# Gates of three branches as 1024-column panels, three of eight k pairs by seven block products, on one core

## What is computed

```python
h = rms_norm(x, norm_g)
u = h @ w_in                       # 7752 columns of branches, then 4 x 2048 columns of gates
...                                # y_a, y_b, y_c, y_m: four mixers of width 512
gate_all = gates.reshape(B, S, N_BRANCH, D_MODEL)
for n, (y, z) in enumerate(((y_a, a_z), (y_b, b_z), (y_c, c_z), (y_m, m_z))):
    branch = y.reshape(B, S, W).astype(dt) * jax.nn.silu(z)
    merged = merged + jax.nn.sigmoid(gate_all[:, :, n]) * (branch @ w_branch[n])
return x + merged @ w_out
```

## Time and profile before

| | |
|---|---|
| median of 3 runs | 3312.29 us (3312.0 to 3312.94) |
| the profiled execution | 3312.98 us, span of its instructions 3311.2 us |
| granted TensorE clock | 0.999 |
| matmuls on PE | 15262, busy 3293.0 us |
| DVE, ACT, POOL busy | 1884.9, 1511.4, 279.0 us |
| DMA | 619.71 MB, mean 187 GB/s |

### The profile page before, as it was taken

The page is one execution under the profiler, slowest core; times in us unless marked ns, Lnnn a source line. Parts: engine busy times, 40 slices in busy tenths (PEclk is TensorE's granted clock), DMA queues, the critical chain, the costliest instruction groups (busy, mean ns, idle before and its releaser), DMA issues.

```text
span 3311.2 us, 39162 instructions
## 1 busy us (share of the span) xinstructions
PE 3293.0 (99%) x15262; PEld 2733.0 (83%) x15262; DVE 1884.9 (57%) x2068; ACT 1511.4 (46%) x1906; POOL 279.0 (8%) x237
## 2 busy tenths in 40 slices
PE   8999999999999999999999999999999999999999
PEld 7888888888888888888888888888888888888887
DVE  5466655555555656555555555575555555555555
ACT  5454445444444444454444445455444444444443
POOL 0111240000000102400000011160000000000000
PEclk9999999999999999999999999999999999999999
DMA  8665555666666655556666675554665666666665
GB/s 296 193 197 165 160 173 164 205 194 193 190 197 204 179 171 159 171 166 188 207 192 189 193 214 172 171 179 141 197 186 189 188 191 192 192 188 191 192 192 167
DMA packets 324279, 619.71 MB, mean 187 GB/s; under 512 B 24960, under 2 KB 29440, under 8 KB 322944
## 3 DMA queue, kind: packets, MB, share of 16 engines
q1 hardware_dynamic: 324096, 617.22, 62.1%
HBM read 609.80 MB, written 7.34 MB: 186 GB/s over the span
## 4 chain that ended last, share of the span: by engine, by line
PE 61%; DVE 0%; issue 0%; ACT 0%; ACTq 0%
PE G L900 57%; PE PT L662 2%; PE PO L773 1%; PE PS L745 1%; PE PS L747 0%; PE G L894 0%; PE PS L800 0%; PE PS L799 0%; PE PO L766 0%; PE PS L821 0%; DVE arena L1194 0%; PE PO L810 0%; ACT w_hi L914 0%; PE PS L822 0%; DVE yz L1260 0%
## 5 line engine op out<-in xcount | busy, mean ns | idle before, releaser
L1166 DVE TENSOR_TENSOR w_lo<-raw,w_hi 128x1024 fp32r<-128x1024 f32 x1132 | 1405.6, 1243 | 1384.7 <-ACT w_hi L914 1363.1
L914 ACT ACTIVATE w_hi<-raw 128x1024 fp32r<-128x1024 f32 x1132 | 1196.5, 1058 | 1688.4 <-PE G L900 1670.8
L900 PE MATMUL G<-w_hi,xh 128*128 128x512 f32 x3200 | 1273.0, 398 | 0.0
L900 PE MATMUL G<-w_hi,xl 128*128 128x512 f32 x3200 | 1249.1, 390 | 0.0
L900 PE MATMUL G<-w_lo,xh 128*128 128x512 f32 x3200 | 1246.7, 390 | 0.0
L900 PEld LDWEIGHTS G<-w_hi,xl 128*128 128x128 f32 x3200 | 601.1, 188 | 128.9
L900 PEld LDWEIGHTS G<-w_hi,xh 128*128 128x128 f32 x3200 | 601.6, 188 | 120.2 <-issue 2.7
L900 PEld LDWEIGHTS G<-w_lo,xh 128*128 128x128 f32 x3200 | 602.2, 188 | 118.9
L900 PE MATMUL G<-w_hi,yh 128*128 128x512 f32 x1304 | 514.9, 395 | 8.7 <-DVE w_lo L1166 8.7
L900 PE MATMUL G<-w_hi,yl 128*128 128x512 f32 x1304 | 509.2, 391 | 0.0
L900 PE MATMUL G<-w_lo,yh 128*128 128x512 f32 x1304 | 508.5, 390 | 0.0
(11 more groups left out here) (163 smaller groups left out, 1370.6 us busy)
## 6 DMA issues: line engine op xcount, KB each, us to landing
raw<-in_w_in SPq DMA_DIRECT2D x624, 512.0 KB, 3.7
raw<-in_w_gate_up SPq DMA_DIRECT2D x176, 512.0 KB, 3.7
raw<-in_w_down SPq DMA_DIRECT2D x88, 512.0 KB, 3.6
raw<-in_w_branch SPq DMA_DIRECT2D x64, 512.0 KB, 3.9
raw<-in_w_out SPq DMA_DIRECT2D x64, 512.0 KB, 4.5
raw<-in_w_mem_kv SPq DMA_DIRECT2D x32, 512.0 KB, 5.7
raw<-in_w_o SPq DMA_DIRECT2D x32, 512.0 KB, 3.7
raw<-in_w_o_dil SPq DMA_DIRECT2D x16, 512.0 KB, 3.7
```

What stands on the lines that cost most here:

```text
L900: mm = M.matmul(G[b % 2][:, t, :], a[:, blk.kk + k, tok], w[:, c % RING, j, :], start=(k == 0 and q == 0), stop=(k == blk.kt - 1 and q == 2))
L914: A(ringed(w_hi, blk, c), ringed(raw, blk, c), ACT.Copy).then_inc(hi_done, 1)
L1166: V.tensor_tensor(ringed(w_lo, blk, c), ringed(raw, blk, c), ringed(w_hi, blk, c).bitcast(F32), ALU.subtract).then_inc(lo_done, 1)
```

## The change

The gates of branches c, m and b are no longer blocks of 512 columns but six panels of 1024 per layer (twelve in all), each followed by its two merge blocks. Gate a and all other blocks stay. A panel has eight k pairs (STEPS). The pairs 0, 2 and 4 (SEVEN) are done by seven block products in place of eight: the operands are split in two by k tile, by half of the tokens and by half of the columns; four of the products take sums of x parts and of weight parts. The other five pairs are done as before, in two rows of 12 matmuls.

A step by seven products has four units: `low` (6 matmuls), `first` (3), `sums13` (6) and `sums24` (6). DVE forms the sums of weights in raw float32 (one 128x1024 and two 128x512 differences, `sums13`, `sums24`), ACT and DVE split them into high and low like other weights. The sums of x are formed by POOL (`x_forms`, three pairs per layer), and split by ACT and DVE (stage `forms`). In the panel PT0, PT1, PS and PO, now one tile X, gather what goes directly into the four quarters of the result, and G0, G1 the four products that are used in more than one quarter. When the last `sums24` is done ACT copies G0 and G1 out (`stem`), DVE combines them (`cross`, four 128x512), adds X at the panel's end (`gather`, two 128x1024), and ACT takes the sigmoid over 1024 columns (`wide_sigmoid`), after which each merge reads its half.

From the first panel of a layer to the end of its last merge the rings have six slots; the two new ones lie over parts of arena, core and bias_row. Where a ring has six slots, ACT and DVE do the side work and the readout of a unit behind the split of the unit six later.

In the side table branch m's heads go from five to four chunks apart, branch b's from r + 146 + 5h to r + 140 + 4h, so that all is over before the first panel; the m_feeds are placed around the end of merge b 2 and b 3. `back` is issued at the end of merge b 3, the load of bias_row at r2 + 8.

The core of the diff:

```diff
+WIDE_RING = 6
+WIDE = 2 * NB
+STEPS = KD // 2
+SEVEN = (0, 2, 4)
...
+                units += [(b, "low", s, k0 + 1), (b, "first", s, k0), (b, "sums13", s, None), (b, "sums24", s, None)]
+            else:
+                units += [(b, "row", 2 * s, k0), (b, "row", 2 * s + 1, k0 + 1)]
...
-            soft(r + 121 + 5 * h, "m", l, h)
+            soft(r + 121 + 4 * h, "m", l, h)
         for h in range(H):
-            c = r + 146 + 5 * h
+            c = r + 140 + 4 * h
             at(c, "b_turn", l, h)
             at(c + 2, "b_qk", l, h)
             at(c + 4, "b_pv", l, h)
             at(c + 6, "norm", "b", l, h)
             at(c + 8, "tail", "b", l, h)
-        for n in range(4):
-            for half in range(2):
-                at(end_of("merge", l, "b", n) + 2 + half, "m_feed", l, n, half)
+        for i in range(len(SEVEN)):
+            at(r + 147 + 2 * i, "forms", l, i)
+        e = end_of("merge", l, "b", 2)
+        for i, c in enumerate((e - 1, e, e, e + 1, e + 1, e + 2, e + 3, e + 4)):
+            at(c, "m_feed", l, i // 2, i % 2)
...
-            return {0: ("m_feed", name[1], 2, 1), 6: ("m_feed", name[1], 3, 1)}.get(s)
+            return ("m_feed", name[1], s // 2, s % 2)
...
+                if R_PREV[r] >= 0:
+                    sp.wait_ge(lo_done, SPLIT_OF[R_PREV[r]] + 1)
+                    if LOADS[R_PREV[r]] in LOAD_SUMS:
+                        sp.wait_ge(sums_done, 2 * LOAD_SUMS[LOADS[R_PREV[r]]] + 2)
+                if r in EXT_LOAD.values():
+                    sp.wait_ge(y_ready, Y_OF["s_pv", "m", blk.name[1], H - 1] + 1)
...
-                sp.wait_ge(y_ready, Y_OF["norm", "b", l, H - 1] + 1)
+                sp.wait_ge(lo_done, SUMS_UNIT[LAST_PANEL[l], SEVEN[-1]] + 1)
...
+            def three(bank, of_h, of_l, c, n, start, stop):
+                cols = slice(n * NB, (n + 1) * NB)
+                M.matmul(bank, of_h, high_of(c)[:, cols], start=start, stop=False)
+                M.matmul(bank, of_h, low_of(c)[:, cols], start=False, stop=False)
+                return M.matmul(bank, of_l, high_of(c)[:, cols], start=False, stop=stop)
+
+            def by_token(k, t):
+                return xh[:, k, t * P:(t + 1) * P], xl[:, k, t * P:(t + 1) * P]
+
+            def by_form(s, f):
+                i = SEVEN.index(s)
+                return form_hi[:, i, f, :], form_lo[:, i, f, :]
+
+            def panel(b, blk):
+                l, n = blk.name[1], PANEL_N[b]
+                if n:
+                    pe.wait_ge(x_banks_free, 2 * n)
+                if b == FIRST_PANEL[l]:
+                    turned(pe, PT_OF["tail", "b", l, H - 1])
+                    pe.wait_ge(ps_free, PS_OF["b_qk", l, H - 1] + 1)
+                    pe.wait_ge(y_ready, Y_OF["norm", "b", l, H - 1] + 1)
+                    pe.wait_ge(forms_done, len(SEVEN) * (l + 1))
+                for c in range(blk.first, blk.end):
+                    _b, what, s, _r = UNITS[c]
+                    first, last = s == SEVEN[0], s == SEVEN[-1]
+                    pe.wait_ge(lo_done, c + 1)
+                    if what == "low":
+                        three(PT[0], *by_token(2 * s + 1, 0), c, 0, first, False)
+                        mm = three(PT[1], *by_form(s, 3), c, 1, first, False)
+                    elif what == "first":
+                        if first:
+                            pe.wait_ge(gm_free[0], blk.before[0])
+                        mm = three(G[0][:, 0, :], *by_token(2 * s, 0), c, 0, first, last)
+                    elif what == "sums13":
+                        three(G[0][:, 1, :], *by_form(s, 0), c, 0, first, last)
+                        if first:
+                            pe.wait_ge(gm_free[1], blk.before[1])
+                        mm = three(G[1][:, 0, :], *by_form(s, 2), c, 1, first, last)
+                    elif what == "sums24":
+                        three(G[1][:, 1, :], *by_form(s, 1), c, 0, first, last)
+                        mm = three(PS, *by_token(2 * s + 1, 1), c, 1, first, False)
+                    else:
+                        end = s == KD - 1
+                        for t, banks in enumerate(((PT[0], PT[1]), (PS, PO))):
+                            for h, bank in enumerate(banks):
+                                mm = three(bank, *by_token(s, t), c, h, bank is PO and c == FIRST_ROW[b], end)
+                    mm.then_inc(mm_done, 1)
+                    between(c)
...
+            def split(c):
+                b, what, s, r = UNITS[c]
+                if r is None:
+                    act.wait_ge(sums_done, 2 * SUMS_N[b, s] + (1 if what == "sums13" else 2))
+                else:
+                    act.wait_ge(raw_landed[R_SLOT[r]], 16 * (R_COUNT[r] + 1))
+                if U_PREV[c] >= 0:
+                    act.wait_ge(mm_done, U_PREV[c] + 1)
+                for l in range(DEPTH):
+                    if c in EXT_FIRST[l]:
+                        act.wait_ge(y_ready, Y_OF["norm", "b", l, H - 1] + 1)
+                        act.wait_ge(o_squared, NORM_OF["norm", "b", l, H - 1] + 1)
+                A(high_of(c)[:, 0:size_of(c)], source_of(c), ACT.Copy).then_inc(hi_done, 1)
+
+            def stem(b):
+                _, l, br, m = BLOCKS[b].name
+                act.wait_ge(mm_done, SUMS_UNIT[b, SEVEN[-1]] + 1)
+                if b == FIRST_PANEL[l]:
+                    freed(act, b - 1)
+                    act.wait_ge(forms_done, len(SEVEN) * (l + 1))
+                else:
+                    act.wait_ge(merge_done, MERGE_N[BLOCKS[b - 1].name] + 1)
+                A(sig_wide[:, 0, 0:NB], G[0][:, 0, :], ACT.Copy)
+                A(five, G[0][:, 1, :], ACT.Copy).then_inc(gm_free[0], 1)
+                A(sig_wide[:, 1, 0:NB], G[1][:, 0, :], ACT.Copy)
+                A(six, G[1][:, 1, :], ACT.Copy).then_inc(gm_free[1], 1)
+
+            def wide_sigmoid(b):
+                by = scale_of(b)
+                act.wait_ge(x_banks_free, 2 * PANEL_N[b] + 2)
+                for t in range(TT):
+                    last = A(sig_wide[:, t, :], sig_wide[:, t, :], ACT.Sigmoid, scale=by[:, t:t + 1])
+                last.then_inc(wide_sig, 1)
...
+                for e in BEHIND[c]:
+                    ended = ENDS.get(e)
                     later = ended is not None and BLOCKS[ended].kind == "bias"
                     if ended is not None and not later:
                         read_out(ended)
-                    if c >= RING:
-                        between(c - RING)
+                    if e in STEM_ENDS:
+                        stem(STEM_ENDS[e])
+                    if e - 1 in ENDS and BLOCKS[ENDS[e - 1]].kind == "panel":
+                        wide_sigmoid(ENDS[e - 1])
+                    between(e)
...
+            def sums13(n, r):
+                for k in (r, r + 1):
+                    dve.wait_ge(raw_landed[R_SLOT[k]], 16 * (R_COUNT[k] + 1))
+                if n >= 2:
+                    dve.wait_ge(lo_done, SUMS_UNIT[SUMS[n - 2]] + 1)
+                q = pair_of(r)
+                V.tensor_tensor(sums[:, n % 2, 0:2, :], q[:, :, 1, :], q[:, 0, :, :], ALU.subtract).then_inc(sums_done, 1)
+
+            def sums24(n, r):
+                q, to = pair_of(r), sums[:, n % 2]
+                dve.wait_ge(sums_done, 2 * n + 1)
+                link(V.tensor_tensor(to[:, 2, :], q[:, 1, 1, :], to[:, 0, :], ALU.subtract))
+                V.tensor_tensor(to[:, 3, :], q[:, 1, 0, :], to[:, 2, :], ALU.subtract).then_inc(sums_done, 1)
+
+            def split(c):
+                b, what, s, r = UNITS[c]
+                if what == "low":
+                    sums13(SUMS_N[b, s], r - 1)
+                elif what == "first":
+                    sums24(SUMS_N[b, s], r)
+                dve.wait_ge(hi_done, c + 1)
+                if U_PREV[c] >= 0:
+                    dve.wait_ge(mm_done, U_PREV[c] + 1)
+                n = size_of(c)
+                V.tensor_tensor(low_of(c)[:, 0:n], source_of(c), high_of(c)[:, 0:n].bitcast(F32), ALU.subtract).then_inc(lo_done, 1)
+
+            def cross(b):
+
+                freed(dve, b)
+                link(V.tensor_tensor(six, sig_wide[:, 0, 0:NB], six, ALU.add))
+                V.tensor_tensor(sig_wide[:, 0, NB:], six, five, ALU.add)
+                link(V.tensor_tensor(sig_wide[:, 1, 0:NB], six, sig_wide[:, 1, 0:NB], ALU.add))
+                V.tensor_tensor(sig_wide[:, 1, NB:], sig_wide[:, 1, 0:NB], five, ALU.add).then_inc(crossed, 1)
+
+            def gather(b):
+
+                pn = PANEL_N[b]
+                dve.wait_ge(mm_done, BLOCKS[b].end)
+                dve.wait_ge(crossed, pn + 1)
+                for t in range(TT):
+                    both = X[:, 2 * t:2 * t + 2, :].rearrange("p a n -> p (a n)")
+                    V.tensor_tensor(sig_wide[:, t, :], both, sig_wide[:, t, :], ALU.add).then_inc(x_banks_free, 1)
...
+                for e in BEHIND[c]:
+                    if e in ENDS:
+                        read_out(ENDS[e])
+                    if e - 2 in STEM_ENDS:
```

(2 more changed lines are left out.)

## The result

The changed kernel took 3340.8 us (median; 3340.3 to 3345.8), the kernel before 3312.1 in the same session: a ratio of 1.009 (95% interval 1.0072 to 1.0107), 28.7 us slower. The forecast was 3329, 16.6 slower. The sign was right, the size short by 12 us. The execution that was profiled is the longest of the four, 3345.8 us with a span of 3344.0; the others are 5 us shorter, and why they differ is part of the answer.

What follows compares the result with a forecast made beforehand. TensorE, busy 3293.0 of 3311.2 us, was taken to bound the kernel. Terms of -24.5 + 17.0 + 6.7 + 10.3 + 7.1 = +16.6 us gave 3329 us (own spread 3320 to 3338), range 3305 to 3346.

Steps and rivals of the forecast that it cites:

- What bounds the kernel: TensorE's row of matmuls: each one removed is worth 0.2267 us, each microsecond of new TensorE wait costs a microsecond.
- Matmuls removed: Twelve panels of 183 matmuls in place of 192: 108 fewer, 24.5 us gained.
- Heads: Branch m, four chunks apart: TensorE waits for DVE's reciprocal, 2.45, 3.6 and 2.45 per layer, 17.0 us lost.
- first panels: First panel of each layer: TensorE waits for G1, still held by merge a 3; 6.7 us lost for two layers.
- other panels: Other ten panels: the bank of G is free at 3.75, wanted at 2.72; 1.03 each, 10.3 us lost.
- feeds: After merge b 2, TensorE waits for DVE's low half for merged's third feed: 7.1 us lost for two layers.
- The rule in bold: Side work of chunk c stands on DVE behind the split that waits for the end of chunk c.
- Work with cover: DVE's panel and merge work, 45.2 of 52.4 us, POOL's forms and the x reload cost zero; 14% of DVE free.
- The clock: TensorE's clock falling in the longest new waits was left out of the sum, as a rival: +15, 3344 us, chance 0.12.
- rival 3: TensorE's clock falls in six new waits over 3 us, 2.5 lost each: +15, 3344 us; chance 0.12.
- Rivals 1 and 2: Panel handovers hidden, only heads cost: 3304.8, chance 0.14; about half of the new waits occur: 3311.9, chance 0.14.
- rival 4: DVE bounds the panels if differences, crosses and gathers cost twice their price: 59 us more, above 3385; chance 0.05.

Runs made afterwards that it cites:

- all three edits: Changed kernel with branch m's score products one chunk later, panels opening with a row step, and merged's feeds one per unit: 3295.8 us, ratio 0.9949.
- doubled sums: The version with all three edits, with each of VectorE's three sums of weights done twice in a row: 3322.6 us in one run.
- the kernel whose heads no longer wait: Changed kernel with branch m's score products three chunks behind the head's start, not two: 3324.3 us, ratio 1.0033.

## Why the prediction was right, and where it was short

**What bounds the kernel.** Right: each matmul less was worth 0.2267 us, and each wait of PE went into the time in full. With all three edits 39.0 us of long distances are gone and the time is 45.0 shorter; nothing had handed them back.

**Matmuls removed.** -24.5, as forecast.

**Heads, first panels, other panels, feeds.** The rule in bold (a stage's work stands on DVE behind the split that waits for its own chunk) named all twenty waits and no other. Forecast and measured, per layer or per panel, measured being the distance of starts less 0.2267:

```
                             forecast            measured
heads, per layer             2.45, 3.6, 2.45     2.24, 3.37, 2.24
first panel of a layer       3.3                 3.12, 3.01
ten other panels             1.03                1.01 to 1.02
feeds, per layer             3.55                3.28
sum                          41.1                38.5
```

**Work with cover.** Right. No wait for rounded weights in the panels, DVE at 260 of 313 us in them, POOL's forms and the x reload unseen. The doubled sums show how near the edge is.

**The clock.** This is the step that failed. The forecast made it a rival of chance 0.12, against which it held that "the four waits of today are up to 2.2 us, with the pace unchanged". The pace is not unchanged there. The trace of the kernel before shows it, behind the second of its two waits of 2.2 us, and I had not looked at that place:

```profile
1299.81 0.46 PE L810 MATMUL PO<-arena,tmp 128*128 128x128 f32 x2 [2.17 <-DVE yz L1260]
...
1300.91 0.67 PE L900 MATMUL G<-w_hi,xh 128*128 128x512 f32 x1
1301.37 0.63 PE L900 MATMUL G<-w_lo,xh 128*128 128x512 f32 x1
1301.80 0.63 PE L900 MATMUL G<-w_hi,xl 128*128 128x512 f32 x1
```

0.43 apart, with a granted clock of 0.51; the same wait in layer 0, at 376.98, has 1.00 behind it:

```profile
1301.00:1304.40 3.40, 3.40 (x11) 2.62 (x10) 1.18 (x2) 0.87 (x5) 1.58 (x3) 0.51 0.82 269
377.00:380.00 3.00, 3.00 (x18) 2.65 (x19) 1.78 (x3) 1.11 (x5) 1.29 (x3) 1.00 0.78 201
```

Had I read both, the rival would have been part of the forecast: a wait of some 2 us may bring a fall, at times. With ten such waits new, and 0.2 us lost per slow matmul in stretches of five to ten, a term of 0 to 20 us and not a case of 0.12. The Trainium skill (TensorE: Matmul & The Clock Gate, HAM oscillation), which the prediction named beside the rival, has idle gaps bring the engine back to 1.2 GHz; the traces agree in part, as 39 of their 69 waits of 2.2 us or more had a fall behind them. It pointed the right way where my reading of the rows did not. The rival's own numbers were wrong in detail: not each wait over 3 us brought a fall (the first panels of the change none), some of 2.2 to 2.5 did, and the size is no constant per wait. Its total, 15 us, is near the 13 of the profiled execution; the usual ones of the change have 5 less, so that nearness is in part luck. In the medians the forecast is short by 12.1 us: the waits were 2.6 less than forecast, the pace gave 5.4 and the small rest 0.4, and the 9 that are left are the clock, which the sum had at nothing.

**The pace.** "The moving operand keeps 512 columns, so I keep the pace" was off by 5.4 us. With 512 columns as before, the matmuls of the panels stood 0.7% (rows) to 1.7% (seven products) further apart than 226.7 ns.

**The chances.** The time of 3340.8 lies in the range, 3 us past the forecast's own spread and 3 short of rival 3; it is the width left for rival 3 that holds it. Rivals 1 and 2 are out (the waits all occur), and rival 4's waits for rounded weights show up only when DVE is given a sixth more.

## What to carry to other kernels

On an engine that is busy 99% of the time, read for every value that it consumes how many instructions stand ahead of the producer in the producer's own queue, counted from the event that releases that queue; here this gave all twenty waits to 0.3 us, and one unit to one step more between producer and consumer removed each or left 0.6 us of it. The block form itself was worth its 24.5 us less 5 of pace; the order of the work around it decided the sign, three small edits turning +28.7 into -17. And expect new waits of TensorE of 2.2 us or more to cost more than their length: six of them, 15.7 us long, cost 25 to 27 in two kernels. Don't multiply, though: ten lost no more to the clock than six.

## What the runs showed of the hardware

TensorE's granted clock fell to half behind waits of 2.2 to 3.6 us, with the engine near 100% busy on either side. Between the first and the last matmul of the thirteen traces (one for each kernel) there are 39 such falls, every one behind a wait of 2.2 us or more. There are 69 such waits: 14 of the 22 over 2.8 us had a fall behind them, and 25 of the 47 of 2.2 to 2.4 us. The 62 shorter waits that I counted (0.4 to 1.7 us) had none. So length within this span hardly decides it. The same place can go either way: neither of the two first-panel waits (3.1 and 3.0 us) had a fall in the change, both had one in the kernel whose heads no longer wait, and of the two old waits of 2.2 us both, one or none had. From execution to execution of one program the mean clock varied between 0.995 and 0.998 and the time with it by 8 us. In the version whose longest wait inside is 2.2 us it was 0.999 to 1.0 and the spread 2 us. What decides whether a given wait brings a fall is open.

Waits already met cost TensorE nothing measurable (3312.0 us with some 4500 more, 3312.2 without). Waking from a real one takes 0.15 us from the releaser's end to the matmul's start, as in the kernel before.
